# The opening of a two-block kernel: constants loaded later, x loaded ahead of c, three weight splits moved from VectorE to GpSimd

## The reference, cut to what matters

```
mod   = silu(c) @ ada_w + ada_b                  # 3 x 1024 numbers: shift, scale, gate
h     = rms_norm(x, norm_pre_w) * (1 + scale) + shift
z     = h @ w_in                                  # 1024 x 6144: u, g_pool, q, f, i, g_h
f     = lb + (1 - lb) * sigmoid(f_pre)            # lb from hgrn_lower_bounds
o     = chunked scan over 8 heads of 128, with causal masks inside a chunk of 64
y     = [pool branch, o] @ w_out; x = x + gate * rms_norm(y, norm_post_w)
```

## Time and profile before

| | |
|---|---|
| median of three executions | 1179.51 us (1178.49 to 1179.69) |
| span of the profiled execution | 1177.2 us from its first to its last instruction |
| TensorE busy | 1128.0 us, 96% of the span |
| VectorE busy | 859.8 us, 73% |
| ScalarE busy | 554.4 us, 47% |
| GpSimd busy | 161.7 us, 14% |
| mean granted TensorE clock | 0.993 |

### The profile page before, as it was taken

One profiled execution on the slowest core, in us unless ns is written; L12 is line 12 of the kernel. 1 busy time (PEld: TensorE's weight loads), 2 busy tenths in 40 slices (PEclk: granted clock), 3 DMA queues, 4 the chain that ended last, 5 costly groups with the idle time before them and its releaser, 6 DMA issues.

```text
span 1177.2 us, 14196 instructions
## 1 busy us (share of the span) xinstructions
PE 1128.0 (96%) x5547; PEld 924.2 (79%) x5547; DVE 859.8 (73%) x1348; ACT 554.4 (47%) x857; POOL 161.7 (14%) x179
## 2 busy tenths in 40 slices
PE   3889999999999999999999999999999999999996
PEld 3678888888888878888886766778888888888885
DVE  5789899999877785666789799886765566655246
ACT  3564645445523343776425676546544434331130
POOL 0044443244423110000100000200000000000001
PEclk9899999999999999999999999999999999999998
DMA  9642323324334566313101012112232232243201
GB/s 377 249 153 100 132 81 144 124 92 144 130 130 170 193 252 252 108 45 144 58 28 47 1 71 72 36 72 72 107 108 101 79 107 107 75 157 143 92 16 72
DMA packets 22651, 136.61 MB, mean 116 GB/s; under 512 B 2576, under 2 KB 2872, under 8 KB 8760
## 3 DMA queue, kind: packets, MB, share of 16 engines
q1 hardware_dynamic: 19936, 128.46, 29.9%
q10 hardware_dynamic: 2648, 7.25, 1.8%
HBM read 133.58 MB, written 2.12 MB: 115 GB/s over the span
## 4 chain that ended last, share of the span: by engine, by line
PE 68%; DVE 18%; ACT 6%; issue 4%; POOL 3%; DMA 2%; DVEq 0%; SPq 0%; ACTq 0%; POOLq 0%
PE PB L185 67%; DVE WL L206 3%; DVE RAW L1412 3%; ACT WH L199 2%; DVE AT L234 1%; DVE UPA L206 1%; DVE SS L214 1%; POOL UPA L206 1%; POOL PTA L206 1%; DVE PTA L206 1%; DVE MPH L1412 1%; DVE XL L214 1%; DMA XL<-in_x 1%; DMA RAW<-in_wstream 1%; DVE HB L231 1%
## 5 line engine op out<-in xcount | busy, mean ns | idle before, releaser
L185 PE MATMUL PB<-HH,WH 128*128 128x512 f32 (+1 forms) x896 | 351.3, 392 | 12.6 <-DVE HL L206 6.8
L185 PE MATMUL PB<-HH,WL 128*128 128x512 f32 (+1 forms) x896 | 340.8, 380 | 0.0
L185 PE MATMUL PB<-HL,WH 128*128 128x512 f32 (+1 forms) x896 | 340.2, 380 | 0.0
L206 DVE TENSOR_TENSOR WL<-RAW,WH 128x1024 fp32r<-128x1024 f32 (+2 forms) x172 | 205.5, 1201 | 179.1 <-ACT WH L199 178.8
L199 ACT ACTIVATE WH<-RAW 128x1024 fp32r<-128x1024 f32 (+2 forms) x172 | 167.5, 979 | 294.2 <-PE PB L185 266.5
L185 PEld LDWEIGHTS PB<-HH,WH 128*128 128x128 f32 x896 | 169.5, 189 | 46.5 <-DVE HL L206 7.7
L185 PEld LDWEIGHTS PB<-HH,WL 128*128 128x128 f32 x896 | 169.3, 189 | 32.4
L185 PEld LDWEIGHTS PB<-HL,WH 128*128 128x128 f32 x896 | 169.7, 189 | 28.5 <-issue 0.5
L214 DVE SCALAR_TENSOR_TENSOR CV<-VP,PC,CV 128x512 f32<-128x512 f32 x120 | 88.0, 777 | 0.7
L206 POOL TENSOR_TENSOR PX<-PX,NPOW 128x2 f32<-128x2 f32 (+2 forms) x7 | 6.5, 935 | 458.9 <-DVE PX L206 421.2
L185 PE MATMUL PB<-WH,AH 128*128 128x512 f32 x176 | 68.5, 389 | 0.0
(11 more groups left out here) (283 smaller groups left out, 1835.9 us busy)
## 6 DMA issues: line engine op xcount, KB each, us to landing
RAW<-in_wstream SPq DMA_DIRECT2D x101, 1024.0 KB, 4.9
EARLY<-in_wstream SPq DMA_DIRECT2D x7, 1024.0 KB, 15.8
RAW<-in_wstream SPq DMA_DIRECT2D x5, 768.0 KB, 4.2
RAW<-in_wstream SPq DMA_DIRECT2D x5, 512.0 KB, 3.5
XL<-in_x SPq DMA_DIRECT2D x2, 1024.0 KB, 8.7
HB<-in_x SPq DMA_DIRECT2D x2, 1024.0 KB, 6.2
out<-XL SPq DMA_DIRECT2D x8, 256.0 KB, 2.0
ROWS<-in_rows ACTq DMA_DIRECT2D x3, 512.0 KB, 8.1
```

The lines of the kernel that those rows point to most:

```text
L185: return self.put(lambda e: e.matmul(o, l, r, start=start, stop=stop, skip_group_check=skip))
L206: return self.put(lambda e: e.tensor_tensor(o, a, b, op))
```

## The change: what it does

- SP issues x, then c, then the weight stream. After item 9 it issues the scan pattern, the masks, parameter columns 40 and up, and the factors; item 10 comes behind them.
- ScalarE issues only the identity and the first 40 parameter columns (`norm_pre_w`, `ada_b`, `hgrn_lower_bounds`, in that order). It squares its tiles of x first and applies silu to c after them.
- VectorE makes its small start of the lower bounds (`LT`) after the diagonals and no longer at its very start.
- The subtractions of blocks 1, 2 and 3 (128x1024 each) are GpSimd's (`first_split`), ahead of its mask copy. VectorE keeps block 0.
- The masks land in HB[8:10], so that ScalarE waits for the mask copy only before head 1's Q; head 0's K waits for the landing of the late loads.

```
+        sp.dma(ROW["c"], A["rows"][:, 0:D]).then_inc(S_.c, "c", by=16)
         for n in range(len(LAY)):
             fetch(n)
+            if n == FIRST_ADA[-1]:
+                sp.dma(SM[:, :], consts[:, 128:640]).then_inc(S_.msk, by=16)
+                sp.dma(MKF, masks[:, :]).then_inc(S_.msk, by=16)
+                sp.dma(PC[:, NPAR_FIRST:], A["params"][:, NPAR_FIRST:]).then_inc(S_.msk, by=16)
+                sp.dma(FAC[:, :], consts[:, 640:704]).then_inc(S_.msk, "m", "rest", by=16)
...
+        def first_split(nb):
+            n, at, size = BLOCKS[nb]
+            g.wait_ge(S_.a_w, nb)
+            g.tt(WL[nb][:, 0:size], raw_of(n)[:, at:at + size], WH[nb][:, 0:size].bitcast(F32), SUB).then_inc(S_.g_w, nb)
+
+        for nb in (1, 2, 3):
+            first_split(nb)
         g.wait_ge(S_.msk, "m")
         g.cp(MK[:, :], MKF).then_inc(S_.g_s, "mk")
...
-        a.dma(ROW["c"], A["rows"][:, 0:D]).then_inc(S_.cs, "c", by=16)
-        a.dma(PC[:, :], A["params"][:, :]).then_inc(S_.par, "par", by=16)
         a.dma(IDN[:, :], consts[:, 0:128]).then_inc(S_.idn, "idn", by=16)
-        a.wait_ge(S_.cs, "c")
-        a.act(ROW["c"], ROW["c"], ACTF.Silu).then_inc(S_.a_s, "c")
-        a.wait_ge(S_.par, "par")
+        a.dma(PC[:, 0:NPAR_FIRST], A["params"][:, 0:NPAR_FIRST]).then_inc(S_.par, "par", by=16)
         for i in (0, 2):
             a.wait_ge(S_.x[i // 2], "x")
             a.act(NORM2[i // 2], XLT[:, i, :], ACTF.Square, ...)
-        a.dma(MKF, masks[:, :]).then_inc(S_.msk, by=16)
-        a.dma(SM[:, :], consts[:, 128:640]).then_inc(S_.msk, by=16)
-        a.dma(FAC[:, :], consts[:, 640:704]).then_inc(S_.msk, "m", by=16)
+        a.wait_ge(S_.c, "c")
+        a.act(ROW["c"], ROW["c"], ACTF.Silu).then_inc(S_.a_s, "c")
+        a.wait_ge(S_.par, "par")
...
         h_low_first(0)
         split(0)
         h_low_first(1)
-        split(1)
         first_dots(1, 0)
         first_dots(1, 1)
         scales(1)
-        split(2)
-        h_low_first(2)
-        split(3)
-        h_low_first(3)
+        h_low_first(2, 3)
```

More of the change, by code:

```diff
@@ L21 @@
 NKEY = NCTX + S
-PARAMS = [("norm_pre_w", 8), ("ada_b", 24), ("pool_scale", 8), ("hgrn_lower_bounds", 8),
+PARAMS = [("norm_pre_w", 8), ("ada_b", 24), ("hgrn_lower_bounds", 8), ("pool_scale", 8),
           ("hgrn_norm_w", 1), ("norm_post_w", 8), ("conv_dw_b_2", 4),
@@ L29 @@
 NPAR = sum(n for _, n in PARAMS)
+NPAR_FIRST = 40
 def stream_layout():
@@ L332, in sem @@
             return Sem(ctx.enter_context(nc.semaphore(name)))
-        self.par, self.idn, self.msk, self.cs = sem("s_par"), sem("s_idn"), sem("s_msk"), sem("s_cs")
+        self.par, self.idn, self.msk, self.cs, self.c = (sem("s_" + z) for z in ("par", "idn", "msk", "cs", "c"))
         self.x = [sem(f"s_x{i}") for i in range(4)]
@@ L341, in __init__ @@
         self.p_sm = sem("p_sm")
-        self.a_w, self.v_w = sem("a_w"), sem("v_w")
+        self.a_w, self.v_w, self.g_w = sem("a_w"), sem("v_w"), sem("g_w")
         self.a_ev, self.v_ev = sem("a_ev"), sem("v_ev")
@@ L355, in vars_of @@
     out = []
-    for z in (sems.par, sems.idn, sems.msk, sems.cs, sems.x, sems.ctx, sems.crow, sems.out, sems.vec, sems.row, sems.raw, sems.early, sems.p_blk, sems.p_sm,
-              sems.a_w, sems.v_w, sems.a_ev, sems.v_ev, sems.a_ax, sems.v_ax, sems.a_h, sems.v_h, sems.v_ada,
+    for z in (sems.par, sems.idn, sems.msk, sems.cs, sems.c, sems.x, sems.ctx, sems.crow, sems.out, sems.vec, sems.row, sems.raw, sems.early, sems.p_blk, sems.p_sm,
+              sems.a_w, sems.v_w, sems.g_w, sems.a_ev, sems.v_ev, sems.a_ax, sems.v_ax, sems.a_h, sems.v_h, sems.v_ada,
               sems.a_s, sems.v_s, sems.g_s, sems.v_st, sems.a_st, sems.g_acc, sems.g_cv, sems.v_cv, sems.a_cv):
@@ L374, in build_in @@
     EV, AX = (S_.a_ev, S_.v_ev), (S_.a_ax, S_.v_ax, S_.v_s)
+    W_LOW = (S_.v_w, S_.g_w)
     IDN = sb("IDN", [128, 128])
@@ L456, in build_in @@
     FS = SS[:, :, :].rearrange("p a n -> p (a n)")
-    MKF = HB[:, 0:2, :].rearrange("p a n -> p (a n)")[:, 0:896]
+    MKF = HB[:, 8:10, :].rearrange("p a n -> p (a n)")[:, 0:896]
     MKv = MK[:, :].rearrange("p (l n) -> p l n", n=128)
@@ L621, in fetch @@
                 if LAY[was][0] == "w":
-                    sp.wait_ge(S_.v_w, LAST_BLOCK[was])
+                    for b in (b for b, (m, _, _) in enumerate(BLOCKS) if m == was):
+                        sp.wait_ge(W_LOW, b)
                 else:
@@ L699, in pool_prog @@
         power(sct(0)[:, 4:8], sct(0)[:, 8:12], 4, "xd")
+        for u in UP:
+            g.memset(u[:, 0:16], 0.0).then_inc(S_.g_s)
+        def first_split(nb):
[4 more added lines that the diff above has]
+            first_split(nb)
         g.wait_ge(S_.msk, "m")
         g.cp(MK[:, :], MKF).then_inc(S_.g_s, "mk")
-        for u in UP:
-            g.memset(u[:, 0:16], 0.0).then_inc(S_.g_s)
         for step in range(-6, 0):
@@ L844, in head @@
             if b == 0:
-                a.wait_ge(S_.g_s, "mk")
                 a.copy(Vb, z).then_inc(S_.a_ev, ("z", h, b))
@@ L855, in head @@
             elif b == 2:
+                if h == 1:
+                    a.wait_ge(S_.g_s, "mk")
                 a.copy(Qb, z).then_inc(S_.a_ev, ("z", h, b))
@@ L904, in act_prog @@
         a.wait_ge(S_.p_blk, 1)
-        a.wait_ge(S_.g_s, "mk")
+        a.wait_ge(S_.msk, "rest")
         a.act(Kb, main.of(("z", 0, 1)), ACTF.Sigmoid).then_inc(S_.a_ev, ("z", 0, 1))
@@ L1427, in lo @@
             v.tt(dst, src, hi.bitcast(F32), SUB).then_inc(S_.v_h, name)
-        v.wait_ge(S_.par, "par")
-        hlb = col("hgrn_lower_bounds", 0, 8)
-        v.tt(LT, hlb, hlb, SUB).then_inc(S_.v_s, "lt")
         for i in (1, 3):
@@ L1462, in h_low_first @@
                 lo(HL[:, k, :], U[k], HH[:, k, :], ("h", k), ("h", k))
+        v.wait_ge(S_.par, "par")
+        hlb = col("hgrn_lower_bounds", 0, 8)
+        v.tt(LT, hlb, hlb, SUB).then_inc(S_.v_s, "lt")
         first_dots(0, 0)
@@ L1564, in hgrn @@
                     .then_inc(S_.v_ax, ("dg", h))
+        v.wait_ge(S_.msk, "rest")
         v.wait_ge(S_.a_s, "lt")
@@ L2190, in first_tile @@
             wh, wl = WH[b], WL[b]
-            pe.wait_ge(S_.v_w, b)
+            pe.wait_ge(W_LOW, b)
             pe.wait_ge(S_.v_h, ("h", k))
```

## The result

The changed kernel takes 1181.09 us (median of 13 executions, 1178.99 to 1182.92) against 1179.51 (13 executions beside it): a ratio of 1.0016, 95% interval 1.0009 to 1.0023, so 1 to 2.7 us more. The profiled execution is the fastest of the thirteen, 1178.99 us with a span of 1177.2, the same span as before. Of the kernels further down, one execution of e8 took 2295.51 us in place of some 1177; the ratio leaves it out.

A forecast was written before the change was run, and what follows sets the result against it. TensorE is 96% busy; the opening is bound by x's landing, then VectorE up to HL(3)'s end. Terms -1.65 - 2.2 - 0.45 + 5.1 = +0.8 on span 1177.2, plus 2.3, were given as 1180.4 us, range 1175.0 to 1183.3.

The forecast's parts named there:

- Part 1, loads: Opening loads: x ahead and small loads gone let the first dots end at 18.0, a gain of 1.65 us.
- Part 2, VectorE's splits: VectorE's opening chain: removing its splits gains 2.2 us before the dots of p = 1 and 0.45 at HL(3), together 2.6.
- Part 3, GpSimd's splits: Dots of p = 1: three GpSimd subtractions of 1.9 us each hold VectorE 1.7 us, a loss of 5.1 us.
- Part 4, the sum: End of HL(3): all terms together move it from 35.78 to 36.6, +0.8 us.
- One for one: Behind 35.83: what moves the end of HL(3) moves the rest equally, as long as VectorE keeps ahead of TensorE.
- the slow clock: TensorE's half-speed stretch in the opening: it stays, cost about 3.3 us, and was left unchanged with +-1.5 us.
- The room for HL(7): Block 1's last matmuls: about 3 us of cover for HL(7), hiding the mask copy's 0.77 us holding of the p = 2 dots.
- GpSimd without holding: Rival, dots of p = 1: GpSimd doesn't hold them, HL(3) ends at 31.6, -4.3 us, 1175.2 us; chance 0.17.
- The dearer holding: Rival, dots of p = 1: each GpSimd subtraction takes 2.8 us and holds 2.6, 1183.1 us; chance 0.18.
- Item 5 landing late: Rival, weight stream: item 5 lands no earlier than 28.05, two holdings on the chain, sum -0.9, 1178.6 us; chance 0.07.

The follow-up runs named there:

- e8: Against e1 (changed loads, all splits on VectorE), split 3 alone moved behind HL(3); median 1177.06 us, ratio to before 0.9978.
- e2: The kernel before with only the three splits moved to GpSimd, ahead of its mask copy, loads as before; median 1183.27 us, ratio to before 1.0030.
- e4: The changed kernel with each of GpSimd's three splits done twice; median 1185.92 us, ratio to before 1.0050.
- e9: The changed kernel with GpSimd doing split 1 alone, splits 2 and 3 back on VectorE around HL(2); median 1177.92 us, ratio to before 0.9990.
- e5: The kernel before with only c issued by SP behind x and its silu behind ScalarE's squares; median 1178.13 us, ratio to before 0.9990.
- e1: The changed kernel with all three splits back on VectorE in their old order, loads and silu staying changed; median 1177.33 us, ratio to before 0.9979.
- e10: The changed kernel with GpSimd doing only split 1, behind A1(1), and VectorE's splits 2 and 3 behind HL(3); median 1179.29 us, ratio to before 0.9991.
- e6: Against e1, VectorE's split 1 moved behind A1(1) and splits 2 and 3 behind HL(3); median 1176.45 us, ratio to before 0.9976.
- e7: e6 with x tile 5 ahead of block 1's first tiles and GpSimd's mask copy behind A1(3); median 1177.37 us, ratio to before 0.9975.

## Why the prediction was right, step by step

The forecast was 1180.4 us, no change or a little slower, and 1181.09 was measured. The mechanism is shown: the trace has the turns, e2 has them without the loads, e4 with more of them and e9 with one. That the number came out so near is in part luck: the loads gave 0.45 us more than forecast and the holdings cost 1.15 us more, and what is left of the two, 0.7, is small.

- **Part 1, loads.** Forecast: x at 9.4, first dots at 13.1, their end at 18.0, gain 1.65 us. In the trace: x at 8.77, dots at 12.54, A1(0) at 17.65 in place of 19.75: 2.1 us. I worked it out from the bytes ahead of each item, and had the masks, pattern and factors (736 KB) at nothing, though before they were issued at 11 to 12.5 us, ahead of item 1's landing at 16.7. With them and all the parameters still in their old place (e5) item 1 lands at 16.0, without them at 15.0; the 219 KB of parameters, which the forecast did count, make 0.5 of that by bytes.
- **Part 2, VectorE's splits.** The dots of p = 1 start right behind HL(1) (22.29), and behind A1(1) HL(2) waits 1.57 us for HH(2) in place of 0.43. As forecast, 2.2 and 0.45. Of the 2.2, 0.77 is the mask copy's and not the split's; at its later place (37.62) the copy is off the chain, and so it is with the loads alone (e1).
- **Part 3, GpSimd's splits.** The placing was right: one after each of three dots. The size was not: 1.9 us for the subtraction and 1.7 for a holding, against 2.36 (e10) and 2.1. The sum of this term is 3.28 + 3.30 + 3.27 - 3 x 1.20 = 6.25 us in place of 5.1, the largest error of the sum. I had extended a line through 128x256 and 128x512, whose rows had float32 outputs and a broadcast input; here both inputs are full and the output is fp32r. Which of these makes the difference was not tried. The estimate of 2.25 us from the Trainium skill ("GPSIMD Engine Reference", section "Elementwise — side-by-side cycle accounting") was the nearer. The page "SBUF — State Buffer" of the Trainium skill (section "SBUF: two separate sides") has the lock for the whole instruction; 2.1 of 2.36 agrees but for the last 0.25.
- **Part 4, the sum.** HL(3): +0.8 forecast, +1.5 measured (37.30 against 35.78), from -2.1 - 2.2 - 0.45 + 6.25 = +1.5. With 1.5 in place of 0.8 the same sum gives 1181.0 us. (As it stands it gives 1180.3: 1177.2 + 0.8 + 2.3; the forecast says 1180.4.) "One for one" does not hold in the trace: 0.86 of the 1.5 reached head 0, since less of TensorE's work lay in the slow clock, and I had left that at zero, with +-1.5. The medians (1 to 2.7 us more) agree better with the whole 1.5. The room for HL(7) was there: it ended at 52.9, and TensorE ran without a gap for 20.72 us, from 36.02, since HL(3) was ready as soon as TensorE had finished with HL(2). WL(2) and WL(3) were never waited for.
- **The rivals.** GpSimd without holding: ruled out by e1 and e2. The dearer holding (2.6): no, 2.1, but the truth lies between it and my 1.7; its condition, 2.2, was missed by little. Item 5 landing late: it landed at 25.0, and e2 shows what else would have happened.

## What to carry to other kernels

Giving an elementwise operation with two inputs to GpSimd relieves VectorE only while VectorE waits for something else; in front of a row of VectorE instructions with two inputs from SBUF, an operation of 1.2 us there becomes a standstill of 2.1 us here. First look for the engine's own waits: behind A1(1) VectorE's own subtraction is free, and split 1 put there (e6) took it off the row of dots without a second engine. HL(3) came 1.9 us sooner than in e1 by it; that the whole kernel gained is not shown. And a change of two parts that comes out near zero is worth taking apart: here -2.5 us and +3.5 us lay on top of each other.

## What the runs showed of the hardware that was not expected

GpSimd and VectorE take strict turns in these traces: with more GpSimd operations ready one behind the other, no VectorE instruction waited for more than one of them (e4, and splits 2 and 3 of the changed kernel), and even the operation of 128x2 waited its 2 us.

TensorE's clock also dips far from the opening, in some profiles only. At 755 to 765 us it stays at full speed in the kernel before; in e6 it does not, with matmuls recorded for all of the ten microseconds in both. Windows of the kernel before and then of e6 (columns as above):

```profile
755.00:765.00 10.00, 10.00 (x62) 8.85 (x61) 6.34 (x19) 6.79 (x9) 1.33 (x1) 1.00 0.02 7
```

```profile
755.00:765.00 10.00, 10.00 (x35) 8.21 (x36) 4.88 (x17) 3.47 (x5) 1.33 (x1) 0.68 0.00 0
```

The price can be read from GpSimd's small power operations: e6 is 3.5 us ahead of the kernel before at 761 us and 0.5 us ahead at 794. The profiles of e2 to e5 and e7 to e10 lose 1.5 to 1.6 us there, those of before, changed and e1 nothing. That, and not the opening, is why the profiled span of e6 (1176.7) lies 3.1 us above e1's (1173.6) although its opening is shorter. One profile says where time goes in a stretch; the verdict on a microsecond needs the medians. What makes the clock dip in one profile and not in another stays open; each profile is one execution of another kernel, so the kernel itself may have a part in it.
